# Sample attention of a decoder step: by kind of head, with gathered keys turned by DVE

## The chip, the cores and the metric

The kernel runs on one core of a Trainium2 chip. The metric is the device time of one execution in microseconds (us). A core has TensorE (PE in the profile, its weight loads PEld), VectorE (DVE), ScalarE (ACT), GpSimd (POOL) and SyncE (SP), which run their own instruction queues in order and meet at semaphores, and 16 DMA engines that all queues share. All data here is float32.

## The reference, cut to what matters

One layer of a decoder is applied to a prompt (256 tokens) and to 8 samples of 8 new tokens, each sample with 1024 past keys that lie in 8 pages of 128 tokens (a page table names them). Half of the attention is stick-breaking ("stick"), 8 heads of 64; half is differential ("diff"), 4 heads with two 64-wide key halves and values of 128. A mixture of experts (top 4 of 32) follows.

```python
# stick: z (heads, queries, keys), only keys before the query count
log_1m = where(mask, log_sigmoid(-z), 0.0)
log_rest = cumsum(log_1m, reverse=True) - log_1m
w = where(mask, exp(log_sigmoid(z) + log_rest), 0.0)      # = sigmoid(z_s) * product of sigmoid(-z_j), j > s
# diff: two softmaxes over z - slope * distance
a = p[:, 0] - lam * p[:, 1]
out = w_or_a @ v
```

The rest is projections, two layer norms, the router and, for each chosen expert, `gate_up` (1024 x 2048) and `down` (1024 x 1024).

## The kernel before, in words

The program is a row of blocks; at the end of each all engines meet.

**Block 1, projection** (L243 to L426). SP loads `w_in` into `ring`. PE projects the 64 sample rows and the first 128 prompt rows, then `turn(n)` (L310) transposes q and k rows of them, 8 turns of 4 transposes, ACT and DVE copying alternate turns out of banks 6 and 7 (`copy_turned`, L368; the sample queries go into `q_all`). Then PE projects the second prompt block (L329 to L332), which frees `ring` row by row (`w_in_used`), and turns that too. As `ring` comes free SP loads the first sample's pages (L255 to L258).

**Block 2, attention** (L486 to L1045). First the samples. One turn of the loop is one sample with both kinds. For each kind 1024 x 512 keys and as many values come as 16 page loads of 256 KB with 2 KB rows (`load_pages`, L208) into `slot[0]` to `slot[7]`, keys of stick in 0 and 1, of diff in 2 and 3, values in 4 to 7. PE transposes every 128x128 block of the keys (`turn_keys`, L583), ACT and DVE copy the results from banks 5 and 6 into `kT` (`copy_bank`, L487; `WHO` deals 22 bank copies per sample to the two), PE multiplies them by `q_now`, in which the queries of a head pair stand block-diagonal (`score_keys`, L597). Stick weights are made in logs: Abs, Exp, Ln on ACT (L794 to L797), max and add, a reversed scan of 1088 on DVE (L944), subtractions, Exp on ACT (L763). Diff weights are a biased maximum on DVE (L903 to L910) and Exp on ACT (L766). PE transposes the weights and multiplies them by the values (`mix_values`, L620, product L639), ACT copies the result, PE turns it (`turn_rows`, L645), DVE stores it into `mixT` (`store_rows`, L885). The order on PE is L660 to L671: the mix of the last sample lies between the key turns of this one. SP's order is L532. After the samples, L545 loads `w_out` and `load_weights` the first expert's weights, as slots come free. Then the prompt's attention runs in 6 units (L681 to L743, L819 to L861, L971 to L1045).

**Block 3** (L1131 to L1390) projects with `w_out`, norms, routes, and ranks tokens by expert. **Block 4** (L1451 on) runs 33 items of 64 slots: POOL gathers the item's rows (`gather`, L1470, 128 rows of 2 KB by indirect DMA), PE multiplies by the streamed weights of the expert (L1530, L1560) from the 12 slots, and SP loads the next expert's into each slot when `w_used` says that it is free.

## Time and profile before

| | us |
|---|---|
| Runs: median (lowest to highest of 3) | 1502.22 (1501.36 to 1503.99) |
| The profiled execution, its own time | 1504.01 |
| Its span, first to last instruction | 1502.2 |
| PE busy | 1317.1 (88%) |
| DVE, ACT, POOL busy | 475.0, 254.3, 56.2 |
| Mean granted TensorE clock | 0.928 of full speed |
| Block 1 | 0 to 135.9 |
| Samples' attention in block 2 | 136.4 to 344.2 |
| Prompt's attention, blocks 3 and 4 | to the end |

The profile gives for each engine what it was busy with and what ended its idle time. DMA rates are of the whole core. A PE row counts two instructions for each float32 product. A granted clock of 1.00 is 2.4 GHz and one of 0.50 is 1.2 GHz; a stretch between has some of both.

### The profile page before, as it was taken

How to read it: one execution, taken by the hardware profiler on the slowest of the kernel's cores; microseconds unless marked ns; L12 is line 12 of the kernel's file. 1: busy time of each engine (PE TensorE's matmuls, PEld its weight loads, DVE VectorE, ACT ScalarE, POOL GpSimd, SP SyncE). 2: the span in 40 equal slices, each digit the busy share in tenths (PEclk: the TensorE clock that was granted, in tenths of full speed). 3: DMA queues.
4: the chain of work that ended last, by engine and by line, in shares of the span. 5: the costliest groups of instructions: out<-in, count | busy, mean ns of one | idle time of the engine just before them, and what ended most of it. 6: DMA issues, size and time to landing. Idle time of an engine off the chain costs nothing.

```text
span 1502.2 us, 20503 instructions
## 1 busy us (share of the span) xinstructions
PE 1317.1 (88%) x7083; PEld 517.9 (34%) x7084; DVE 475.0 (32%) x809; ACT 254.3 (17%) x436; POOL 56.2 (4%) x90
## 2 busy tenths in 40 slices
PE   8997888874697999999899999999999999999994
PEld 3344555553344323222232222222322222222221
DVE  0002656565556221223222231222122222312225
ACT  0003666665422000000000000000000000000001
POOL 0000000000000000000000000000000000000000
PEclk9999999996595999999899999999999999999996
DMA  9144779896114999999999999599999999999991
GB/s 388 39 165 175 272 279 338 292 384 277 45 67 162 410 418 417 415 418 417 403 389 416 418 417 418 219 393 419 416 416 418 418 418 416 417 418 418 417 416 71
DMA packets 119411, 507.97 MB, mean 338 GB/s; under 512 B 13492, under 2 KB 13620, under 8 KB 85464
## 3 DMA queue, kind: packets, MB, share of 16 engines
q1 hardware_dynamic: 116016, 496.85, 82.9%
q0 software_dynamic: 3232, 10.49, 1.9%
q8 instruction: 16, 0.26, 0.1%
q10 hardware_dynamic: 136, 0.28, 0.0%
q14 instruction: 11, 0.09, 0.0%
HBM read 502.33 MB, written 5.24 MB: 338 GB/s over the span
## 4 chain that ended last, share of the span: by engine, by line
PE 53%; DVE 6%; DMA 4%; SPq 3%; ACT 1%; issue 1%; ACTq 0%; DVEq 0%; POOLq 0%; POOL 0%
PE psum L1530 28%; PE psum L1560 17%; PE psum L1500 6%; DMA arena<-in_w_gate_up 4%; SPq L226 3%; DVE arena L1680 1%; PE psum L1550 1%; ACT arena L1614 1%; DVE arena L1681 1%; DVE arena L1688 1%; DVE arena L1684 1%; PE psum L1509 1%; PE psum L1581 0%; DVE arena L1741 0%; DVE arena L1738 0%
## 5 line engine op out<-in xcount | busy, mean ns | idle before, releaser
L1530 PE MATMUL psum<-arena 128*64 128x512 f32 x2112 | 478.0, 599 | 4.7 <-issue 2.3
L1651 DVE SCALAR_TENSOR_TENSOR arena<-psum,arena 128x1024 f32<-128x1024 f32 (+2 forms) x132 | 128.0, 1008 | 592.5 <-PE psum L1500 592.1
L1560 PE MATMUL psum<-arena 128*64 128x512 f32 x1056 | 275.7, 682 | 22.7 <-ACT arena L1614 22.7
L1530 PEld LDWEIGHTS psum<-arena 128*64 128x64 f32 x2112 | 145.6, 137 | 326.1 <-issue 308.5
L1560 PEld LDWEIGHTS psum<-arena 128*64 128x64 f32 x1056 | 82.5, 155 | 195.0 <-issue 164.1
L1612 ACT ACTIVATE arena<-arena 128x512 f32<-128x512 f32 x33 | 20.8, 630 | 580.3 <-DVE arena L1680 580.3
L1500 PE MATMUL psum<-arena 64*128 64x512 f32 (+1 forms) x396 | 107.5, 632 | 0.9 <-ACT arena L1618 0.9
L593 PE MATMUL psum<-arena 128*128 128x128 f32 x512 | 74.4, 285 | 17.0 <-ACT arena L506 8.1
L283 PE MATMUL psum<-arena 128*128 128x512 f32 x192 | 85.9, 603 | 0.0
L506 ACT ACTIVATE arena<-psum 128x512 f32<-128x512 f32 x112 | 61.9, 574 | 69.6 <-PE psum L593 41.1
L1618 ACT ACTIVATE arena<-psum 128x512 f32<-128x512 f32 x33 | 19.7, 597 | 281.7 <-PE psum L1560 281.7
L593 PEld LDWEIGHTS psum<-arena 128*128 128x128 f32 x512 | 55.8, 143 | 32.3 <-ACT arena L506 14.1
L1680 DVE TENSOR_SCALAR arena<-psum 128x512 f32<-128x512 f32 x33 | 22.8, 692 | 137.8 <-PE psum L1530 137.8
L1509 PE MATMUL psum<-arena 1*64 1x512 f32 x272 | 37.0, 612 | 29.1 <-DVE arena L1681 28.2
L504 DVE COPY arena<-psum 128x512 f32<-128x512 f32 (+1 forms) x64 | 39.5, 639 | 66.7 <-PE psum L593 43.4
L1500 PEld LDWEIGHTS psum<-arena 64*128 64x128 f32 (+1 forms) x396 | 26.5, 167 | 79.4 <-issue 79.4
L283 PEld LDWEIGHTS psum<-arena 128*128 128x128 f32 x192 | 36.3, 193 | 49.5 <-issue 49.5
L351 DVE COPY arena<-psum 128x512 f32<-128x512 f32 (+2 forms) x18 | 11.2, 645 | 121.4 <-PE psum L335 41.7
L1471 POOL COPY small_i<-small_i 128x1 int32 (+1 forms) x34 | 6.2, 182 | 1056.9 <-PE psum L1492 886.4
L1474 POOL DMA_INDIRECT arena<-x_rows,small_i x34 | 40.2, 1183 | 26.8 <-POOL small_i L1471 26.8
L626 PE MATMUL psum<-arena 128*128 128x128 f32 x144 | 22.9, 286 | 15.4 <-ACT arena L763 11.3
L639 PE MATMUL psum<-arena 128*32 128x128 f32 x1152 | 36.2, 281 | 0.0
(197 smaller groups left out, 862.1 us busy)
## 6 DMA issues: line engine op xcount, KB each, us to landing
arena<-in_w_gate_up SPq DMA_DIRECT2D x256, 1024.0 KB, 17.0
arena<-in_w_down SPq DMA_DIRECT2D x128, 1024.0 KB, 13.9
arena<-in_cache_sb_k SPq DMA_DIRECT2D x64, 256.0 KB, 4.3
arena<-in_cache_diff_k SPq DMA_DIRECT2D x64, 256.0 KB, 8.0
arena<-in_cache_sb_v SPq DMA_DIRECT2D x64, 256.0 KB, 5.2
arena<-in_cache_diff_v SPq DMA_DIRECT2D x64, 256.0 KB, 6.9
arena<-in_w_in SPq DMA_DIRECT2D x8, 1536.0 KB, 20.2
arena<-in_w_out SPq DMA_DIRECT2D x4, 1024.0 KB, 18.1
```

The source lines that it names most:

```text
L226: sp.dma_start(dst, src).then_inc(w_loaded[s], 16)
L283: return nc.tensor.matmul(psum[:, bank_of[n], :], xT[:, k, b * P:(b + 1) * P], ring[:, col:col + 512], start=(k == 0), stop=(k == KD - 1))
L504: nc.vector.tensor_copy(dst, src).then_inc(copied["dve"], 1)
L506: nc.scalar.activation(dst, src, ACT.Copy).then_inc(copied["act"], 1)
L593: ins = nc.tensor.transpose(psum[:, 5 + j % 2, h * P:(h + 1) * P], slot[s][:, at:at + P], ident)
L1474: pool.indirect_dma_start(xg, None, x1_dram, bass.IndirectOffsetOnAxis(ap=idx_now, axis=0)).then_inc(gathered, 16)
L1500: ins = nc.tensor.matmul(psum[0:nt, banks[h], :], scatter[r, t0:t0 + nt], y_rows[r, :], start=True, stop=True)
L1509: ins = nc.tensor.matmul(psum[64 * h:64 * h + 64, n, :], ones_rows[32 * n:32 * n + 1, :], bias_row[32 * n:32 * n + 1, h * 512:h * 512 + 51 ...
L1530: ins = nc.tensor.matmul(psum[64 * h:64 * h + 64, n, :], x_k, slot[k][:, col:col + 512], start=False, stop=(k == KD - 1))
L1560: ins = nc.tensor.matmul(psum[64 * h:64 * h + 64, 4, :], h_k, slot[s][:, col:col + 512], start=(k == 0), stop=(k == KD - 1))
L1651: ins = nc.vector.scalar_tensor_tensor(out=r, in0=psum[0:nt, banks[h]:banks[h] + at_once, :], scalar=item_gate[0:nt, b, col], in1=r, op0=A ...
L1680: nc.vector.tensor_scalar(gate_in, psum[:, 0, :], LIMIT, None, ALU.min).then_inc(gate_clamped, 1)
```

## The change

The sample attention of block 2 is written anew, and block 1 prepares for it. The rest of the kernel is the same, except for a few constants in `consts` and places of buffers.

- **Units.** Instead of 8 turns with both kinds there are 16 units, `UNITS`: first 8 samples of stick, then 8 of diff. They are written out, not looped.
- **Keys.** A unit's keys (2 MB) come by one indirect DMA on POOL's queue, `load_keys`: 128 indices, each one contiguous run of 8 tokens, 16 KB, into one partition. Partition p then holds tokens 8p to 8p+7, so a block of 32 partitions holds a quarter of the keys. The indices are made in block 1 from the page table. There are two buffers, `K_raw`; unit u+2 is loaded after `keys_turned` says that u is turned.
- **Turning.** DVE transposes 32x32 blocks (`turn_keys(u, h)`: two instructions of 1024 elements per partition for each half h, four for a unit), from contiguous rows of 32, and writes them 8 elements (32 bytes) apart into `T`. PE's key transposes, the 16 bank copies and `kT` go.
- **Queries.** Block 1 spreads q and k of the samples over 32-row parts with products: sample turns n = 0 to 7 replace four turns of four transposes; a q turn has 32 products of 64 columns, a k turn 8. ACT's `place` puts them block-diagonal over the four quarters.
- **Scores** of a unit are 16 products of 264 columns (256 past and 8 own keys) in 2 banks, one for each h.
- **Stick weights.** ACT makes sigmoid(-z) and sigmoid(z) (4 instructions of 264); DVE scans the first as a product over 264 columns, twice; PE turns the quarters' totals, three small DVE operations multiply them up, PE turns them back, two DVE operations of 264 finish.
- **Diff weights.** The bias comes as a product; DVE takes the maximum, PE and DVE join it over the quarters, ACT takes Exp with the maximum as its bias.
- **Mixing.** 6 transposes instead of 9 and 36 products of 128 columns, as before. Values still come as 8 page loads with 2 KB rows on SP, two buffers; a unit's values load after the mix two units back.
- POOL makes the run indices in block 1 from 8 small DMAs of the page table; `w_out` is loaded at unit 4.

The core of it (the rest of the two kernels' block 2 is replaced in the same manner):

```diff
+        def load_keys(pool, u):
+            y, b = UNITS[u]
+            pool.indirect_dma_start(K_raw[u % 2], None, key_runs[y],
+                                    bass.IndirectOffsetOnAxis(ap=runs[:, b:b + 1], axis=0)).then_inc(keys_loaded[u % 2], 16)
...
                 def turn(n):
-                    b, i = (2, 0, 1)[n // 4], n % 4
-                    nt = BLOCKS[b][1]
-                    for h in range(4):
-                        ins = nc.tensor.transpose(psum[:, 6 + n % 2, h * P:h * P + nt],
...
+                    if n < 8:
+                        i = n // 2
+                        for j in range(8):
+                            at = i * 512 + 32 * (4 * (j // 2) + 2 * (n % 2) + j % 2)
+                            for c in range(3 * (i % 2), 4):
+                                ins = nc.tensor.matmul(psum[32 * c:32 * c + 32, 6 + n % 2, j * SAMPLES:(j + 1) * SAMPLES],
+                                                       qk_rows[0:64, 2, at:at + 32], ident[0:64, 0:64], start=True, stop=True)
...
-                for n in range(2, 8):
+                for n in range(2, 12):
...
             @block.sync
...
+                for u in range(2, N_UNITS):
+                    sp.wait_ge(mixed, u - 1)
+                    load_values(sp, u)
+                    load_own(u)
...
             @block.gpsimd
...
+                for u in range(2, N_UNITS):
+                    pool.wait_ge(keys_turned, 2 * u - 2)
+                    load_keys(pool, u)
...
             @block.tensor
...
+                score_unit(0, 0)
+                score_unit(0, 1)
+                for u in range(N_UNITS):
+                    if u + 1 < N_UNITS:
+                        score_unit(u + 1, 0)
+                    if u:
+                        turn_rows(u - 1)
+                    join_quarters(u)
+                    turn_weights(u)
+                    if u + 1 < N_UNITS:
+                        score_unit(u + 1, 1)
+                    mix_values(u)
+                turn_rows(N_UNITS - 1)
...
             @block.scalar
...
+                for u in range(N_UNITS):
+                    more = u + 1 < N_UNITS and UNITS[u + 1][0] == 0
+                    if UNITS[u][0]:
+                        exponents(u)
+                    if more:
+                        sigmoids(u + 1, 0)
+                    copy_weights(u)
+                    if more:
+                        sigmoids(u + 1, 1)
+                    if u + 2 < N_UNITS:
+                        place(u + 2)
+                    rows(u)
...
             @block.vector
...
+                def turn_keys(u, h):
+                    if h == 0:
+                        dve.wait_ge(keys_loaded[u % 2], 16 * (u // 2 + 1))
+                    if u:
+                        dve.wait_ge(scored, 2 * (u - 1) + h + 1)
+                    raw = K_raw[u % 2].rearrange("p (s g x r) -> p s g x r", s=RUN, g=4, x=4)
+                    turned = T[:, 8 * h:8 * h + 8, 0:QUARTER].rearrange("p (g d) (c s) -> p s g d c", d=2, s=RUN)
+                    for d in range(2):
+                        ins = nc.vector.transpose(turned[:, :, :, d, :], raw[:, :, :, 2 * h + d, :])
...
+                for u in range(N_UNITS):
+                    y = UNITS[u][0]
+                    if u + 1 < N_UNITS:
+                        turn_keys(u + 1, 0)
+                    if y == 0:
+                        sticks(u)
+                    else:
+                        maxima(u)
+                    if u:
+                        store_rows(u - 1)
+                    if u + 1 < N_UNITS:
+                        turn_keys(u + 1, 1)
+                    if y:
+                        factors(u)
+                store_rows(N_UNITS - 1)
```

## Rows read from the trace of the kernel before

**Rows 1.** The page: the chain that ended last, shares of the span.
```profile
PE 53%; DVE 6%; DMA 4%; SPq 3%; ACT 1%; issue 1%; ACTq 0%; DVEq 0%; POOLq 0%; POOL 0%
PE psum L1530 28%; PE psum L1560 17%; PE psum L1500 6%; DMA arena<-in_w_gate_up 4%; SPq L226 3%; DVE arena L1680 1%; PE psum L1550 1%; ACT arena L1614 1%; DVE arena L1681 1%; DVE arena L1688 1%; DVE arena L1684 1%; PE psum L1509 1%; PE psum L1581 0%; DVE arena L1741 0%; DVE arena L1738 0%
```

**Rows 2.** Time windows: span, busy us (and count) of PE, PEld, DVE, ACT, POOL, granted clock, DMA share, GB/s.
```profile
216.08:241.28 25.20, 20.54 (x277) 13.94 (x277) 14.23 (x26) 16.04 (x26) 0.40 (x1) 1.00 0.92 328
```

**Rows 3.** Timeline (start us, us, engine, line): the ends of the turns, projections and sample stage.
```profile
79.20 0.71 PE L315 MATMUL psum<-arena 64*128 64x64 f32 x8
...
86.45 42.55 PE L283 MATMUL psum<-arena 128*128 128x512 f32 x96
...
136.42 1.43 PEld L593 LDWEIGHTS psum<-arena 128*128 128x128 f32 x8 [2.90 <-issue]
...
216.08 2.04 PE L610 MATMUL psum<-arena 128*32 128x512 f32 x16
...
241.28 2.04 PE L610 MATMUL psum<-arena 128*32 128x512 f32 x16
...
344.04 0.19 DVE L896 TENSOR_TENSOR arena<-psum,arena 128x32 f32<-128x32 f32 x1
```

**Rows 4.** Groups by line and form, 0 to 560 us: xcount | busy us, mean ns | idle before.
```profile
L593 PE MATMUL psum<-arena 128*128 128x128 f32 x512 | 74.4, 285 | 17.0 <-ACT arena L506 8.1 <-issue 4.5 <-DVE arena L504 3.7
L506 ACT ACTIVATE arena<-psum 128x512 f32<-128x512 f32 x104 | 59.7, 597 | 66.3 <-PE psum L593 41.1 <-PE psum L626 25.1
...
L504 DVE COPY arena<-psum 128x512 f32<-128x512 f32 x56 | 38.0, 690 | 66.7 <-PE psum L593 43.4 <-PE psum L626 23.1
...
L944 DVE TENSOR_TENSOR_SCAN arena<-arena 128x1088 f32<-128x1088 f32 x8 | 19.4, 2426 | 0.3
...
L949 DVE TENSOR_TENSOR arena<-psum,arena 128x1024 f32<-128x1024 f32 x8 | 9.7, 1215 | 0.0
...
L994 DVE TENSOR_TENSOR_SCAN arena<-arena 128x256 f32<-128x256 f32 x8 | 4.9, 673 | 0.1
...
L837 ACT ACTIVATE arena<-arena 128x256 f32<-128x256 f32 x8 | 4.0, 496 | 3.9 <-DVE arena L1022 3.9
...
L1039 DVE SCALAR_TENSOR_TENSOR arena<-arena 128x256 f32<-128x256 f32 x4 | 1.8, 482 | 0.1
```

**Rows 5.** Timeline: one mix of 36 products; one round trip ACT, PE, DVE.
```profile
235.79 2.17 PE L639 MATMUL psum<-arena 128*32 128x128 f32 x72
...
343.45 0.33 PE L647 MATMUL psum<-arena 128*128 128x128 f32 x1 [0.49 <-ACT arena L757]
...
343.81 0.19 DVE L894 COPY arena<-psum 128x32 f32<-128x32 f32 x1 [2.55 <-PE psum L647]
```

**Rows 6.** Two single lines: strided and contiguous reductions of 256 elements.
```profile
L1667 DVE TENSOR_REDUCE arena<-arena x3: 590/600/609, 484.0 to 488.2; 128x64 f32<-128x256 f32 x2, 64x64 f32<-64x256 f32 x1
...
L1367 DVE TENSOR_REDUCE arena<-arena x3: 411/420/421, 466.3 to 471.6; 128x8 f32<-128x256 f32 x2, 64x8 f32<-64x256 f32 x1
```

**Rows 7.** DMA view, 165 to 318 us, in 40 slices: page loads.
```profile
GB/s 246 393 373 392 389 380 30 163 293 400 391 388 386 172 248 336 400 389 387 387 46 291 313 403 388 387 382 29 252 360 399 388 387 380 26 245 378 398 387 388
```

**Rows 8.** Windows while 8 KB rows are loaded: columns as in rows 2.
```profile
540.00:700.00 160.00, 150.72 (x678) 47.29 (x676) 40.01 (x54) 9.72 (x16) 6.85 (x10) 0.97 1.02 417
```

**Rows 9.** Chain in order of time: the first gather of rows.
```profile
477.88 3.19 DMA arena<-x_rows,small_i
```

**Rows 10.** Short windows around a fall and a rise of the clock: columns as in rows 2.
```profile
132.00:135.00 3.00, 1.51 (x11) 0.86 (x9) 1.79 (x4) 1.05 (x2) 0.00 (x0) 1.00 0.02 5
...
138.00:141.00 3.00, 2.22 (x12) 1.62 (x11) 0.11 (x1) 1.84 (x4) 0.55 (x2) 0.66 0.32 122
...
357.00:360.40 3.40, 2.94 (x14) 1.82 (x10) 2.81 (x7) 1.47 (x4) 0.00 (x0) 0.50 1.03 422
...
408.00:411.40 3.40, 3.40 (x12) 0.99 (x9) 0.00 (x0) 0.00 (x0) 0.00 (x0) 0.75 0.89 281
```

**Rows 11.** Timeline: one mix after the fall.
```profile
335.10 3.56 PE L639 MATMUL psum<-arena 128*32 128x128 f32 x72
```

More of the change, by code:

```diff
@@ L70, in constants @@
     put("pneg", np.where(k < 128 + i, 0.0, NEG))
[L72 to L73 removed]
+    c = (i % 32) // 8
+    group, quarter, q = i // 32, (i % 32) // 8, i % 8
+    n = np.arange(KEYS_Q)[None, :]
+    own = n >= QUARTER
     slope = np.array(SLOPES)[group]
[L75 to L80 removed]
+    key = np.where(own, PAST + n - QUARTER, QUARTER * quarter + n)
+    seen = np.where(own, (quarter == 3) & (n - QUARTER <= q), True)
+    put("abias", np.where(seen, slope * (key - (PAST + q)), NEG))
+    n = np.arange(DEC_T)[None, :]
+    put("smask", np.where((quarter == 3) & (n < q), 0.0, NEG))
+    row_c = (j % 32) // 8
+    put("fold", np.concatenate([(j // 32 == group) & (j % 8 == q) & (row_c % 2 == h) for h in range(2)], axis=1))
+    put("run", i % (PAGE // RUN))
+    put("minus", -1.0 * (i == np.arange(2)[None, :]))
     put("slot", j % SLOTS)
@@ new lines, in exponents @@
+                def exponents(u):
+                    b = UNITS[u][1]
+                    act.wait_ge(max_spread, b + 1)
+                    nc.scalar.activation(minus_max, psum[:, SIDE[u % 2], P:P + 2], ACT.Copy).then_inc(max_copied, 1)
+                    act.wait_ge(max_copied, b + 1)
+                    act.wait_ge(w_turned, u)
+                    for h in range(2):
+                        ins = nc.scalar.activation(W[u % 2][:, h, :], z_of(u, h), ACT.Exp, bias=minus_max[:, h:h + 1],
+                                                   accum_out=row_sum[:, h:h + 1])
+                        if h == 0:
+                            own.mark(ins)
+                    ins.then_inc(w_ready, 1)
+                    act.wait_ge(w_ready, u + 1)
+                    act.sem_inc(z_used, 1)
@@ new lines, in copy_weights, with rows @@
+                def copy_weights(u):
+                    act.wait_ge(w_turned, u + 1)
+                    if u >= 2:
+                        act.wait_ge(mixed, u - 1)
+                    own.mark(nc.scalar.activation(w_past[u % 2], psum[:, W_BANK, :], ACT.Copy))
+                    own.wait()
+                    nc.scalar.activation(w_own[u % 2][0:DEC_T, :], psum[0:DEC_T, SIDE[u % 2], 256:512], ACT.Copy
+                                         ).then_inc(w_copied, 1)
+                def rows(u):
+                    y, b = UNITS[u]
+                    act.wait_ge(mixed, u + 1)
+                    if u:
+                        act.wait_ge(o_turned, u)
@@ L805, in _ @@
-                turn(0, first=True)
-                own.leave(1)
-                with act.Fori(1, DEC_B) as b:
-                    turn(b)
-                    own.leave(DEC_B - 1)
-                skip("act", act, DEC_B, (0, 1, 2, 3))
-                weights(DEC_B - 1, 0)
-                banks("act", act, DEC_B, (4, 5, 6))
-                skip("act", act, DEC_B, (7, 8, 9, 10))
-                weights(DEC_B - 1, 1)
-                rows(DEC_B - 1, 0)
-                banks("act", act, DEC_B, (11, 12, 13))
@@ L817, in _, with place @@
-                rows(DEC_B - 1, 1)
+                    nc.scalar.activation(o_rows, psum[:, O_BANK, 0:P], ACT.Copy, scale=row_factor[:, 0:1] if y else 1.0
+                                         ).then_inc(o_copied, 1)
+                def place(u):
+                    y, b = UNITS[u]
+                    if u:
+                        act.wait_ge(scored, 2 * u)
+                    for i in range(4):
+                        r = slice(32 * i, 32 * i + 32)
+                        nc.scalar.activation(q_blocks[u % 2][r, :, 8 * i:8 * i + 8], spread[r, 2 * y, :, 8 * b:8 * b + 8],
+                                             ACT.Copy).then_inc(blocks_ready, 1)
+                    nc.scalar.activation(T[96:128, :, QUARTER:KEYS_Q], spread[96:128, 2 * y + 1, :, 8 * b:8 * b + 8], ACT.Copy
+                                         ).then_inc(blocks_ready, 1)
```

664 lines of the change are left out of this document (273 added, 391 removed).

## The prediction

> **What bounds it now.** I read the page's chain first. It names only lines of block 4 [rows 1]: from there on the core lives on streamed weights, at 417 GB/s with PE busy 94% of the time [rows 8]. The change does not touch that work, and its start is the end of what lies before. So the question is how long blocks 1 and 2 take; whatever the samples' attention gains or loses moves everything behind it by as much, since the first expert's weights and `w_out` come long before they are used.
>
> The timeline gives the stage: turns from 79.20, the second projection from 86.45, the samples' attention from 136.4 to 344.2 [rows 3]. One sample takes 241.28 - 216.08 = 25.2 us [rows 3], so one kind of one sample, a unit of the new kernel, takes 12.6. The window of that turn has PE busy 20.5 of 25.2 us, ACT 16.0, DVE 14.2, DMA 0.92 at 328 GB/s [rows 2]. PE is the longest, and its idle time and the copies' are waits on each other: the key and weight transposes L593 (74.4 us in the stage) wait for ACT and DVE bank copies, which wait for the transposes [rows 4]. DMA is near behind: loads run at about 390 GB/s where they run, with holes between the bursts [rows 7].
>
> A measurement of this kernel can tell about 0.2% (3 us) from no change.
>
> **What goes.** Per sample 64 key transposes on PE (74.4 us over 8 samples, 9.3 each), the 16 key bank copies of 0.60 to 0.69 us on ACT and DVE, the scan of 2.43 us, and the log arithmetic [rows 4]. What stays per unit on PE: scores, 16 products of 264 columns instead of 8 of 512, so the same 2.04 us as L610 [rows 3]; the mix, 36 products, 2.17 us as L639 [rows 5]; 6 transposes and side products, 1.3; sum with round trips about 6.5 us against some 10 before.
>
> **What comes on DVE.** A unit has 4 transposes of 1024 elements. No row shows one. Below: a one-pass operation of 1024 took 1.22 us (L949) [rows 4], so t = 1.22. Above: the slowest rate per element in the trace is the scan's, 2426 ns for 1088 [rows 4], so about 2.3 us. I take t = 1.25 with 1.9 as the near worry: reading with steps of 256 bytes cost L1667 600 ns where L1367, contiguous, took 420 for the same 256 elements [rows 6], 0.7 ns more per element, which on 1024 gives 1.9; the transpose writes in steps of 32 bytes, but reads rows, so it is nearer to the contiguous row. A stick unit has besides two scans of 264 (673 ns for 256, so 1.4), two round trips to PE of 0.4 us each (PE's L647 starts at 343.45, DVE's next at 343.81), three small operations of 0.2, two operations of 0.45 and two small stores [rows 4, 5]: 1.4 + 0.8 + 0.6 + 0.9 + 0.4, with gaps 4.3 us. DVE needs 4t + 4.3 = 9.3 us for a stick unit. A diff unit has a maximum over 528 (0.7), a round trip, two small operations, stores and factors, about 2.5, so 4t + 2.5 = 7.5.
>
> The Trainium skill ("Vector Engine (DVE) Microarchitecture Reference", The reshape front-end) says that the transpose sustains one element per cycle per lane. By it t is at the lower end; no run yet shows it.
>
> **PE in that loop.** In a stick unit PE has, from the moment the keys' second half is turned: scores 1.0, mix 2.2, scores of the next unit's first half 1.0, row transpose 0.3, and only then the quarter totals, at about 5.0; DVE could ask for them at 2.5 + 1.4 = 3.9. So DVE waits about 1 us and the loop is near 10.3. In a diff unit the chain maximum, join, Exp (two of 0.5, L837 [rows 4]), transposes 1.3, two ACT copies of about 1.0 and factors takes DVE from one unit to the next in about 9.5. ACT itself has 4 to 5 us of work in either.
>
> **What the loads allow.** A unit is 2.1 MB of keys and 2.1 MB of values. Values still have 2 KB rows, at 390 GB/s [rows 7] 5.4 us. For runs of 16 KB there is no row: the 8 KB rows of the weights went at 417 GB/s [rows 8], 5.0 us. The bytes alone give 10.4 us per unit. But the load is also a loop: keys of u+2 are issued when u is turned, and DVE's next transpose needs them one period later. The gather of 256 KB landed 3.2 us after its issue [rows 9], 0.6 of it data, after about 1 us of POOL, so some 3.6 us are fixed. With 5.0 for the data if nothing else runs, and 10.0 if values take half throughout, a period lies between 8.6 and 13.6. Values start some 3 to 4 us after the keys are issued, when PE has mixed; keys have had 1 us or so alone and share the rest, which gives 11.3 in a stick unit and up to 12.4 in a diff unit if the two queues share evenly, 10.4 if keys get more. I take P = 11.5 for a unit.
>
> **Block 1.** Eight sample turns take the place of four. A q turn has 32 products of 64 columns. The nearest row, L639's 72 instructions in 2.17 us, 30 ns each [rows 5], gives 64 instructions 1.9 us; a k turn, 8 products on one group, is like the 8 instructions of L315 in 0.71 [rows 3], twice, 1.4. That is 4 x 1.9 + 4 x 1.4 = 13.2 us for what took about 4 with its waits, so +9, between +4 (some of it under copies) and +14 (the clock low, as it was for part of 138 to 141 [rows 10]). It is all on the path: PE does the turns before the second projection, and no loads can start before that. The 8 small table loads on POOL lie under `w_in`'s load, where PE is busy; nothing, and 2 us if they hold back the first x rows. The removed clearing of `v_new` is hidden too.
>
> **The sum,** against the profiled execution's own 1504.0 (span 1502.2; 1.8 above the median of the runs). The stage begins at 136.4 + 9 = 145.4. DVE turns unit 0 (4t = 4.9), and iteration 0 starts at 150. It takes 10, then 14 iterations of P, then the last unit from its turned keys: scores 1.2, maximum and join 1.7, Exp 1.8, transposes 1.3, copies 1.0, mix 2.2, rows and store 1.2 = 10.4. 150 + 10 + 14 x 11.5 + 10.4 = 331.4, against 344.2: 12.8 less. 1502.2 - 12.8 = 1489.4 as a median, say 1489. The break-even period is P = 12.4.
>
> **Rivals.**
> *Loads at full rate.* If the gather's long runs go first where the queues share, P is 10.5, and the stage ends at 150 + 10 + 147 + 10.4 = 317.4, 26.8 less: 1475. For it: values have nearly two periods of slack, keys one. Against: nothing in the trace shows two big streams at once. With block 1 at +4 it would be 1470. Chance 0.23.
>
> *The transposes are slow* (slower than before). At t = 2.3 DVE needs 13.5 for a stick unit and 11.7 for a diff unit, seven of each in the middle 176; the start is 4.3 later and iteration 0 two longer: 150 + 4.3 + 12 + 176.4 + 10.4 = 353, 9 more: 1511. At t = 1.9 it is 11.9 and 11.5 (loads) and hardly moves the forecast. The balance is at t = 2.1. For it: the strided row [rows 6]. Against: that row strides its reads. Chance 0.14.
> The Trainium skill ("Advanced Engine Details and Errata", SBUF Cachelines) says that accesses that go to another 16-byte line each time are slower; steps of 32 bytes do that. By this rule t is above 1.22; row L1667 agrees for reads, at 1.7 times per element; for writes no row shows it.
>
> *The clock falls in the stage* (slower). Before, PE was busy 81% and had 1.00 throughout [rows 2]. It fell after PE had been busy half the time (132 to 135, then 0.66), and stayed at 0.50 while busy 2.94 of 3.4; it rose only after a fully busy stretch [rows 10]. In the new stage PE is busy some 6.5 of 11.5 us. At 0.50 the mix takes 3.56 instead of 2.17 [rows 5, 11] and scores a microsecond more each half; in a stick unit PE then comes to the totals at 8.5 instead of 5, and the period is about 13. 150 + 11 + 182 + 12 = 355, 11 more: 1513. For it: those rows. Against: gaps in the loop are under 2 us each, and the loop has a microsecond or two of slack under the loads. A partly low clock stays inside the forecast. Chance 0.12.
>
> *The gather does not keep up* (the change doesn't do what it says): if runs of 16 KB share with values from the start, P = 13.6, and 150 + 10 + 190 + 10.4 = 361, 17 more: 1519. Chance 0.07.
>
> **Numbers.** The forecast, P of 11 to 12, has 0.44 and runs from 1482 to 1497. The range takes it, the fast case and most of the two slow ones up to P = 13: 1467 to 1513. Slower by over 0.2% holds most of the three slow cases: 0.28. Within 0.2%: 0.06. Faster 0.66.
>
> **What would show it.** Transposes near 1.25 us each, 64 of them; DVE waiting for keys (DMA) once per unit, not for PE; stage periods of 11.5 in both kinds, about equal; DMA share above 0.9 with no holes of 30 GB/s; the second projection starting near 95 instead of 86.45; blocks 3 and 4 unchanged in length. The forecast is wrong if units of the two kinds differ by more than 1.5 us (then an engine's chain sets them), if a transpose is above 2 us, if the granted clock is near 0.50 in the stage, or if the gathers land later than 10 us after issue.

## The result and the profile after

The changed kernel takes 1538.8 us in the median of four runs (1532.2 to 1544.0) beside 1503.1 of the kernel before on the same chip: 1.0235 times as long, 95% interval 1.0215 to 1.0254. The forecast was 1489, the range 1467 to 1513. It is slower, by 36 us, where 14 us less were foretold. The profiled execution has a span of 1533.2, 31.0 more than before. TensorE's first product of the prompt starts at 376.69 us; before it was 343.71, and the sample stage ended near 344.2 [rows 3]. So all of it lies ahead of there, in the sample stage and block 1.

The page's chain looks as it did [rows 1], with nothing of the stage in it; the groups say more (page, line, engine, out<-in, count | busy us, mean ns | idle before):

```profile
L836 DVE STREAM_TRANSPOSE arena<-arena 128x1024 f32<-128x1024 f32 x64 | 123.0, 2019 | 2.8 <-DVE arena L920 1.3
...
L550 PE MATMUL psum<-arena 128*32 128x264 f32 x512 | 50.9, 532 | 38.8 <-DVE arena L836 31.5
...
L605 PE MATMUL psum<-arena 128*16 128x128 f32 x1024 | 46.6, 359 | 11.6 <-issue 10.4
```

The 64 transposes take 2.02 us each, not 1.25; TensorE waits 31.5 us for them. The timeline of one stick unit, from one group of transposes to the next:

```profile
203.23 7.59 DVE L836 STREAM_TRANSPOSE arena<-arena 128x1024 f32<-128x1024 f32 x4 [0.16 <-DVE arena L920]
...
206.12 4.47 SPq L220 DMA_DIRECT2D arena<-in_cache_sb_v  x8
207.22 1.99 PE L550 MATMUL psum<-arena 128*32 128x264 f32 x16 [3.54 <-DVE arena L836]
...
209.66 2.79 PE L605 MATMUL psum<-arena 128*16 128x128 f32 x64
...
212.72 1.10 PE L550 MATMUL psum<-arena 128*32 128x264 f32 x16
...
214.51 0.18 DVE L872 COPY arena<-psum 2x32 f32<-2x32 f32 x1 [2.60 <-PE psum L562]
...
216.91 2.02 DVE L836 STREAM_TRANSPOSE arena<-arena 128x1024 f32<-128x1024 f32 x1 [0.16 <-DVE arena L920]
```

It is a ring through two engines. Two transposes (3.8 us) must end before TensorE can score the second half, and it is idle 3.54 us until then. Behind that wait the same 16 score products take 1.99 us that take 1.10 a few microseconds later, and the mix takes 2.79 where it took 2.17 before [rows 5] and takes 1.94 in this kernel at the full clock (below). VectorE in turn waits 2.60 us for the quarter totals. The windows of this unit and of the whole stage (columns as in [rows 2]):

```profile
203.23:216.91 13.68, 8.28 (x120) 4.94 (x118) 10.40 (x14) 4.05 (x12) 0.94 (x1) 0.75 0.74 278
```
```profile
144.00:360.00 216.00, 138.55 (x1737) 81.86 (x1737) 156.49 (x189) 64.16 (x194) 14.19 (x17) 0.73 0.77 289
```

The granted clock is a mean of 0.73 of its upper level (2.4 GHz) over the stage, so it spends a good half of it at 1.2 GHz; the loads run 0.77 of the time at 289 GB/s. Before it was 1.00 and 0.92 [rows 2]. Neither an engine nor the loads are busy throughout: in a stick unit the ring of waits is the bound.

A third loss stands out in the order of units. Their periods, from the own-key product of one mix to the next, are 13.8, 13.7, 13.7, 13.7, 23.2, 14.0, 13.7 for the stick units, and 10.3 to 14.5 for the softmax ones. The timeline around the long one, SyncE's queue and TensorE:

```profile
194.65 0.71 SPq L499 DMA_DIRECT2D arena<-arena  x1
206.12 4.47 SPq L220 DMA_DIRECT2D arena<-in_cache_sb_v  x8
210.63 0.73 SPq L499 DMA_DIRECT2D arena<-arena  x1
211.41 4.04 SPq L514 DMA_DIRECT2D arena<-in_w_out  x4
225.63 5.85 SPq L220 DMA_DIRECT2D arena<-in_cache_sb_v  x8
```
```profile
236.49 0.60 PE L553 MATMUL psum<-arena 128*128 128x8 f32 x2
245.99 1.27 PE L605 MATMUL psum<-arena 128*16 128x128 f32 x20 [8.90 <-issue]
```

Values of the sixth unit are issued at 225.63, behind 4 MB of `w_out`, and TensorE stands 8.90 us. While it stands the loads run at 404 GB/s (window 225.6 to 246), so it waits for bytes that were asked for late. And the line that reads the page numbers into SyncE's registers, which the forecast did not price (line view, ns min/median/max):

```profile
L216 SPq TENSOR_LOAD <-in_page_table_ptr x16: 1003/2500/4477, 116.3 to 353.5; - x16
L216 SPq TENSOR_LOAD <-in_page_table x16: 873/886/3728, 118.7 to 355.5; - x16
```

They stand behind the wait for the mix. The third mix frees its tile at 199.1 us and the values are issued at 206.12; for the next three units issue comes 12.8, 13.2 and 4.3 us after the mix. Of the 12.8, SyncE spends 2.7 on the end of `w_out`'s issue (to 215.45) and 7.8 in these two loads (4.03 and 3.73). The start of the stage (timeline, all engines):

```profile
143.97 7.57 DVE L836 STREAM_TRANSPOSE arena<-arena 128x1024 f32<-128x1024 f32 x4 [0.32 <-PEq L250]
...
149.66 1.99 PE L550 MATMUL psum<-arena 128*32 128x264 f32 x16 [7.33 <-ACT arena L758]
...
153.16 3.85 DVE L836 STREAM_TRANSPOSE arena<-arena 128x1024 f32<-128x1024 f32 x2 [0.23 <-DVE arena L853]
...
157.17 1.99 PE L550 MATMUL psum<-arena 128*32 128x264 f32 x16 [3.02 <-DVE arena L836]
...
171.24 0.41 PE L609 MATMUL psum<-arena 8*16 8x128 f32 x8
```

From the first transpose to the end of the first mix pass 27.7 us, with nothing of another unit to overlap. Last, block 1 (timeline):

```profile
16.93 1.98 PE L299 MATMUL psum<-arena 128*64 128x512 f32 x4 [5.06 <-DMA arena<-in_w_in]
```

The first product with `w_in` starts at 16.93; before it was 12.14. The sample turns start at 83.17 (79.20 in [rows 3]) and the second projection at 95.49 (86.45).

### The profile page after: what moved, and what is told of

Same layout as the page of the kernel before. It is cut to its first block, busy times and chain, and to the rows that moved or that the text cites. A ratio compares the mean times of both kernels' runs of the same rounds, so it can differ in the third digit from the quotient of the medians.

```text
span 1533.2 us, 19561 instructions
## 1 busy us (share of the span) xinstructions
PE 1305.1 (85%) x7091; PEld 500.1 (33%) x7092; DVE 520.8 (34%) x804; ACT 192.2 (13%) x418; POOL 71.5 (5%) x108
## 4 chain that ended last, share of the span: by engine, by line
PE 52%; DVE 6%; DMA 4%; SPq 3%; ACT 1%; issue 1%; DVEq 0%; POOLq 0%; POOL 0%; ACTq 0%
PE psum L1503 27%; PE psum L1533 16%; PE psum L1473 6%; DMA arena<-in_w_gate_up 3%; SPq L233 3%; DVE arena L1653 1%; PE psum L1523 1%; ACT arena L1587 1%; DVE arena L1654 1%; DVE arena L1661 1%; DVE arena L1657 1%; PE psum L1482 1%; PE psum L1554 1%; DVE arena L1714 0%; DVE arena L1711 0%
## 5 line engine op out<-in xcount | busy, mean ns | idle before, releaser
L1503 PEld LDWEIGHTS psum<-arena 128*64 128x64 f32 x2112 | 145.4, 137 | 324.6 <-issue 309.7
L836 DVE STREAM_TRANSPOSE arena<-arena 128x1024 f32<-128x1024 f32 x64 | 123.0, 2019 | 2.8 <-DVE arena L920 1.3
L550 PE MATMUL psum<-arena 128*32 128x264 f32 x512 | 50.9, 532 | 38.8 <-DVE arena L836 31.5
L605 PE MATMUL psum<-arena 128*16 128x128 f32 x1024 | 46.6, 359 | 11.6 <-issue 10.4
L363 DVE COPY arena<-psum 128x512 f32<-128x512 f32 (+3 forms) x18 | 11.8, 677 | 126.6 <-PE psum L299 41.3
L1591 ACT ACTIVATE arena<-psum 128x512 f32<-128x512 f32 x33 | 19.7, 598 | 280.0 <-PE psum L1533 280.0
L289 PEld LDWEIGHTS psum<-arena 128*128 128x128 f32 x192 | 35.8, 190 | 48.1 <-issue 48.1
L605 PEld LDWEIGHTS psum<-arena 128*16 128x16 f32 x1024 | 37.1, 129 | 22.8 <-issue 15.8
L550 PEld LDWEIGHTS psum<-arena 128*32 128x32 f32 x512 | 17.2, 137 | 61.4 <-issue 38.6
L584 PE MATMUL psum<-arena 128*128 128x128 f32 x64 | 14.7, 326 | 20.7 <-ACT arena L720 11.9
## 6 DMA issues: line engine op xcount, KB each, us to landing
arena<-in_w_down SPq DMA_DIRECT2D x128, 1024.0 KB, 14.1
```

The source lines that it names most:

```text
L289: return nc.tensor.matmul(psum[:, bank_of[n], :], xT[:, k, b * P:(b + 1) * P], ring[:, col:col + 512], start=(k == 0), stop=(k == KD - 1))
L550: ins = nc.tensor.matmul(z_of(u, h)[32 * g:32 * g + 32, :], q_blocks[u % 2][:, j, :], T[:, j, :], start=(y == 0 and d == 0), stop=(y == 1 ...
L605: nc.tensor.matmul(psum[32 * g:32 * g + 16, O_BANK, 0:P], w_past[n][:, r:r + 16], V_raw[n][:, pg * 512 + g * P:pg * 512 + (g + 1) * P], st ...
L836: ins = nc.vector.transpose(turned[:, :, :, d, :], raw[:, :, :, 2 * h + d, :])
L1503: ins = nc.tensor.matmul(psum[64 * h:64 * h + 64, n, :], x_k, slot[k][:, col:col + 512], start=False, stop=(k == KD - 1))
```

## Experiments

Sixteen kernels ran. E is the changed kernel, 1538.8 us. All are medians; each was measured beside the kernel before, which was between 1501.9 and 1503.0, and a bracket with two ratios is the 95% interval of the time over that. E's own is 1.0215 to 1.0254. Differences whose intervals overlap are not shown by the times alone.

**What a transpose costs.** Added once, behind the last unit's scores, e.g.:

```diff
+ own.link(nc.vector.transpose(wide[:, 0:1024], src))
...
+ own.link(nc.vector.transpose(wide[:, 0:1024].rearrange("p (a c s) -> p a s c", a=4, s=8),
+                              src.rearrange("p (a b r) -> p a b r", a=4, b=8)))
```

> The changed kernel with nine VectorE operations added once, in the 16th unit, on 128 x 1024 floats, each waiting for the one before and writing to a tile that nobody reads any more; nothing that is computed changes. They are: (1, 2) a 32x32-block transpose with dense read and dense write, twice; (3) with the elements of a written row 2 floats apart; (4) 4 apart; (5) 8 apart with two blocks interleaved in each destination; (6) 8 apart with all eight interleaved, as the kernel's own; (7) a dense write with a read 8 apart; (8) a dense copy; (9) a copy in the layout of (6). If the step of the writes is what made the transposes slow: (1, 2) near 1.1 us, a rise with the step up to 2.0 us at (5) and (6), (7) near 1.1 to 1.25, and (9) slower than (8) too. If the transpose of 32x32 blocks of floats is slow by itself: (1) to (7) all near 2.0 us, and (8, 9) below 1.25. If the interleaving of eight blocks costs, not the step: (5) well below (6). Time: some 10 to 15 us above the changed kernel, near 1550.

One run, 1548.5 us. The timeline on VectorE, (1) to (9) in order:

```profile
365.37 1.25 DVE L897 STREAM_TRANSPOSE arena<-arena 128x1024 f32<-128x1024 f32 x1 [1.89 <-PE psum L550]
366.66 1.25 DVE L898 STREAM_TRANSPOSE arena<-arena 128x1024 f32<-128x1024 f32 x1
367.94 1.25 DVE L899 STREAM_TRANSPOSE arena<-arena 128x1024 f32<-128x1024 f32 x1
369.22 1.98 DVE L900 STREAM_TRANSPOSE arena<-arena 128x1024 f32<-128x1024 f32 x1
371.23 2.02 DVE L901 STREAM_TRANSPOSE arena<-arena 128x1024 f32<-128x1024 f32 x1
373.29 2.01 DVE L902 STREAM_TRANSPOSE arena<-arena 128x1024 f32<-128x1024 f32 x1
375.33 2.01 DVE L903 STREAM_TRANSPOSE arena<-arena 128x1024 f32<-128x1024 f32 x1
377.37 0.70 DVE L904 COPY arena<-arena 128x1024 f32<-128x1024 f32 x1
378.10 1.09 DVE L905 COPY arena<-arena 128x1024 f32<-128x1024 f32 x1
```

Dense, 1.25 us. With a step of 2 floats (8 bytes) the same; with 4 floats (16 bytes) 1.98, and 8 cost no more than 4. Interleaving does not matter ((5) and (6) agree), and, against what was expected, a stepped read (7) costs as much as a stepped write. The copy pays too, 1.09 for 0.70. So it is the step, on either side. On the written side 8 bytes are free and 16 are not; on the read side only 32 were tried. The Trainium skill ("Advanced Engine Details and Errata", SBUF Cachelines) speaks of 16-byte lines of which two accesses are needed for full speed: the trace agrees, with 8 bytes free and 16 bytes dear, for writes too. The Trainium skill gives "one element per cycle per lane" for the transpose ("Vector Engine (DVE) Microarchitecture Reference", The reshape front-end); the trace does not bear it out for every layout, with 1.25 us for 1024 elements dense and 1.98 to 2.02 stepped.

**Dense keys, three ways.** The tile holds column s*33 + c in place of 8*c + s, own keys at c = 32:

```diff
- turned = T[:, 8 * h:8 * h + 8, 0:QUARTER].rearrange("p (g d) (c s) -> p s g d c", d=2, s=RUN)
+ turned = T[:, 8 * h:8 * h + 8, :].rearrange("p (g d) (s c) -> p s g d c", d=2, s=RUN)[:, :, :, :, 0:32]
```

In the first kernel TensorE undoes the order as it reads: `T[:, j, :].rearrange("p (s c) -> p c s", s=RUN)`.

> The tile of turned keys holds column s*33 + c in place of 8*c + s, so that the transposes write 32 floats in a row, and the score products read the tile with a step of 33 floats; the computation is the same. If the 8-float step of the writes made the transposes slow: from 1.98 us to between 1.1 and 1.25 us, two of four in a row end 1.7 us earlier, TensorE's idle time of 3.5 us before the second half of the scores shrinks to under 2, a stick unit goes from 13.7 us to about 11.5 to 12, and the time is 1517 to 1526 us. If the transposes are slow whatever the step: they stay at 1.98 and the time within 2 us of 1538. If TensorE reads the stepped tile slower, its score halves go over 1.99 us and eat the gain: time 1530 or more with fast transposes. If the loads bound the stage, the DMA share is at 0.95 or more and the units stay near 13 us with fast transposes.

1535.6 us (1.0205 to 1.0245), 3 us less than E, which is no difference beside the intervals. Transposes and scores (line view, then the timeline):

```profile
L836 DVE STREAM_TRANSPOSE arena<-arena x64: 1202/1205/1249, 143.2 to 353.8; 128x1024 f32<-128x1024 f32 x64
```
```profile
203.67 2.15 PE L550 MATMUL psum<-arena 128*32 128x264 f32 x16 [2.07 <-DVE arena L836]
...
209.51 2.11 PE L550 MATMUL psum<-arena 128*32 128x264 f32 x16
```

The transposes are at 1.205, but the step has moved to TensorE: its 32 score halves take 67.7 us, 2.12 each at either clock, where those of E take 50.9 (1.10 or 1.99 each). The unit is still 13.6 us. So the step goes to the engine that can take it, ScalarE, whose sigmoids read the scores from a bank:

```diff
- nc.scalar.activation(keep[:, h, :], z_of(u, h), ACT.Sigmoid, scale=-1.0)
+ nc.scalar.activation(by_run(keep[:, h, :]), z_in_order(u, h), ACT.Sigmoid, scale=-1.0)
```

> The changed kernel with the dense layout and ScalarE's stepped reads alone, w_out where the change has it. e5_dense_z, which also loads w_out last, stands 26 us under the changed kernel, and the late w_out alone 10 us. If the two add up: 16 us under the changed kernel, 1521 to 1525 us, with one long unit of 22 us or more. If faster units only run into the same late values: 1528 or more.

1525.7 us (1.0136 to 1.0171): 13 us less than E. The sigmoids take 392 ns (391 in E), a read of a bank in steps of 33 floats is free here. Units: 13.0, 11.8, 13.9, 13.0, 24.5, 13.0, 12.7, and 10.0 to 13.9. With `w_out` last:

> Two edits of the changed kernel: the turned keys in the layout s*33 + c, and w_out loaded after the last values. Unlike the earlier dense version TensorE reads the tile in a row, so the scores come out in that order, and ScalarE's two sigmoids (and the exponentials) read them from the bank with a step of 33 floats and write them in the order of the keys; the computation is the same. If the 2.11 us of a score half in the earlier dense version came from TensorE's stepped read: it is back at 1.10 us at the full clock (1.99 behind a wait), the transposes stay at 1.2, a stick unit takes 12.0 to 12.6 us, and the time is 1514 to 1521 us. If ScalarE reads a bank with such a step slower: its sigmoids go over 0.39 us and give back up to 1 us a unit: 1521 to 1527. If the loads bind the stage beside this: DMA share over 0.9 and 12.7 us or more a unit with idle TensorE and VectorE before keys or values: 1524 to 1528.

1512.6 us (1.0048 to 1.0089), but from 1509.0 to 1523.4 between runs; the profiled one has a unit of 20.6 us in the softmax half, where the mix waited 7.24 us for values that SyncE issued late.

**Where `w_out` stands.** On E alone, `if u == 4:` becomes `if u == N_UNITS - 1:`.

> The four 1 MB loads of w_out are issued after the values of the last unit in place of after those of the fifth; the computation is the same. If they stood ahead of the values of the sixth unit and made the one stall of 9.6 us (237 to 246 us): that unit goes from 23.3 us to near 13.7, the later ones keep 11 to 14, and the time is 1528 to 1531 us. If the stage is bound by the bytes that it loads: the units get longer elsewhere and the time stays within 2 us of 1538. If the second block then waits for w_out, its start moves later and gives back up to 10 us: time 1538 or more.

1528.6 us (1.0149 to 1.0203), 10 us less; all seven stick periods are 13.5 to 13.8.

**Page numbers.** First read earlier, still from DRAM, on e5_dense_z:

```diff
+ pages = page_numbers(u)
  sp.wait_ge(mixed, u - 1)
- load_values(sp, u)
+ load_values(sp, u, pages)
```

> The same as e5_dense_z with the eight page numbers of a unit's values read into SyncE's registers before its wait for the mix and not behind it. If that reading, 4 to 7 us behind the wait, makes the values late: they are issued within 1 us of the mix that frees their tile, the mixes of the softmax units wait less for them, and the time is 3 to 10 us under e5_dense_z. If the values land in time anyway or the bytes bind: within 2 us of it.

1510.7 us (1.0037 to 1.0070; runs 1509.3 to 1514.6): 2 us less than e5_dense_z, which a measurement cannot tell from nothing, though no unit of its profile is over 13.0. The values were not issued within 1 us of the mix, as the expectation had it, but 0.2 to 9.8 us after it: SyncE issues the eight loads (4 to 5 us), then reads the next numbers (3.1 and 1.4 us in the median), and that fills its time in a unit. Then loaded once into SBUF, alone on E:

```diff
+ sp.dma_start(small_i[0:1, 0:64], a["page_table"]...).then_inc(numbers_loaded, 16)
...
- a["page_table"][b:b + 1, :], engines=[mybir.EngineType.SP], min_val=0,
+ small_i[0:1, 8 * b:8 * b + 8], engines=[mybir.EngineType.SP], min_val=0,
```

> The changed kernel with the page numbers read from SBUF alone. If the register loads behind the wait are half of the stall of 9.6 us: the values of a unit are issued 3 to 5 us earlier, the unit of 23.3 us falls to 18 to 20, and the time is 1531 to 1536 us. If w_out ahead of the values is the whole of it: within 2 us of 1538.

1525.1 us (1.0139 to 1.0176), 13.7 us less than E: more than expected, and as much as the dense keys. Values are issued 3.0 to 6.0 us after the mix, in E 4.3 to 13.2. The loads to registers (line view) and SyncE's timeline:

```profile
L217 SPq TENSOR_LOAD <-small_i x16: 532/692/988, 116.1 to 342.9; - x16
```
```profile
200.28 4.67 SPq L221 DMA_DIRECT2D arena<-in_cache_sb_v  x8
...
205.76 1.95 SPq L518 DMA_DIRECT2D arena<-in_w_out  x4
213.52 9.16 SPq L221 DMA_DIRECT2D arena<-in_cache_sb_v  x8
```

One load of 0.7 us takes the place of two that sum to 3.4 in the median and to 8 at worst. Values of the sixth unit are issued from 213.52, not 225.63, and with `w_out` still ahead of them the long unit is 15.6 us, not 23.2. So `w_out` and the late issue made the stall together: with `w_out` last the unit takes 13.7, with values asked for earlier 15.6. An estimate: 4 MB are 10 us of loading at the rate of [rows 8], and early values can wait them out. The Trainium skill ("DMA: Bandwidth & Descriptors", Latency and other measured facts) has a floor of about 600 ns for such a register load. The traces do not bear it out as a floor: from SBUF the least here is 532, and in block 4 of E SyncE's line L1430 takes 275 ns in the median of 31. From DRAM in the busy stage the first of the two takes 2500.

**The clock.** Products that nobody reads fill TensorE's wait in each stick unit:

```diff
  turn_weights(u)
+ if u < 8:
+     for _ in range(8):
+         nc.tensor.matmul(psum[:, 2 * ((u + 1) % 2) + 1, KEYS_Q:BANK], ident, tab[:, 0:BANK - KEYS_Q], ...)
  if u + 1 < N_UNITS:
      score_unit(u + 1, 1)
```

> Eight products of 128x128 with 248 columns that nobody reads are added on TensorE in each of the eight stick units, where it waits for the second half of the turned keys; they write an unused part of a bank. If the falling clock behind that wait costs time: the granted clock in the stick units goes from 0.75 to 1.00, the mix from 2.79 to 2.17 us, the score half from 1.99 to near 1.1, the unit from 13.7 to 12 to 12.7 us, and the time is 1526 to 1532 us. If VectorE alone sets the unit: the clock rises, the units stay at 13.7 and the time within 2 us of 1538. If the added products run into the arrival of the keys, the units get longer by up to 1 us each: 1540 to 1546.

1535.7 us (1.0202 to 1.0263), no gain: the clock rose (0.87 in the stick stretch), scores and mix took 1.10 and 1.94 us, but eight were too many:

```profile
203.36 5.20 PE L629 MATMUL psum<-arena 128*128 128x248 f32 x16
208.49 1.10 PE L550 MATMUL psum<-arena 128*32 128x264 f32 x16
```

They end at 208.5; the keys, whose transposes began at 203.07, were ready near 207. With five:

> The changed kernel with five added products in each stick unit in place of eight, nothing else. The eight took 5.2 us in a wait of 3.5 us and made the scores about 1.6 us late. If the clock theory holds: the five take 3.2 us and end with the wait, the score half takes 1.1 us, the mix 1.94 us, the stick unit 11.7 to 12.1 us (from 13.7), and the time is 1525 to 1530 us. If the loads bind at that pace: the units stay over 12.5 us and the time over 1532.

1532.6 us (1.0161 to 1.0232), 6 us less than E in the median, with intervals that overlap. The units show the gain, 12.0 to 12.3 us in place of 13.7, until the values are late; then come 14.1 and 27.5. On e5_dense_z, three:

> The same as e5_dense_z with three products of 128x128 with 248 columns added in each of the eight stick units where TensorE waits for the second half of the turned keys; nobody reads them. If the clock behind that wait still costs time: the score half at 1.1 in place of 1.99, the mix at 1.94 in place of 2.8, a stick unit 1.0 to 1.8 us shorter than without them, near 11 us, and the time 7 to 12 us under e5_dense_z, about 1508. If the loads bind by then: the units go no lower than those of e5_dense_z, with the DMA share over 0.9, and the time stays within 3 us of it.

1516.6 us (1507.7 to 1523.3), inconclusive: units of 11.1 and 11.0, then 14.2, and one of 21.6 in the softmax half.

**Block 1.** The small table loads on POOL after `w_in`, on e8_early: `pool.wait_ge(w_sem[KD - 1], 16)` ahead of them.

> The same as e8_early (dense turned keys, w_out last, page numbers read early), and POOL issues its eight small loads of the page table only when the last part of w_in has landed. In the changed kernel's trace the first product with w_in starts at 16.93 us and not at 12.14 as before, the loads move 160 GB/s in the first 10 us and not 285, and SyncE needs 6.99 us and not 4.33 to issue w_in. If the page-table loads do that: the first product is back near 12.2 us, the turns of the sample rows start near 79 us in place of 84, and the time is 4 to 5 us under e8_early's, near 1506. If it is something else in the first block: no difference, and the time within 2 us of e8_early's 1510.7.

```profile
79.20 5.56 PE L329 MATMUL psum<-arena 64*32 64x64 f32 x260
```

The turns start at 79.20, as before the change, 4.8 us earlier than in e8_early. The first 10 us load 288 GB/s (160 in E). The median, 1509.1, gained only 1.6, less than the intervals can tell, with runs between 1501.9 and 1515.9. In the profiled one, the slowest, units of 16.2, 13.8 and 14.0 us gave it back. Then fewer, larger turns (on e8_early; a q turn's 32 products become 8, from a fourfold copy of the queries):

```diff
- for c in range(3 * (i % 2), 4):
-     ins = nc.tensor.matmul(psum[32 * c:32 * c + 32, ...], qk_rows[0:64, 2, at:at + 32], ident[0:64, 0:64], ...)
+ src = qk_rows[0:64, 2, at:at + 32] if i % 2 else q_four[0:64, 4 * at - 1024 * i:4 * at - 1024 * i + P]
+ ins = nc.tensor.matmul(psum[96 * (i % 2):128, ...], src, ident[0:64, 0:64], ...)
```

> The same as e8_early, and the queries of the samples are copied four times side by side (one copy each by ScalarE and VectorE behind their copies of the projection, beside other products), so that one product of 64x128 writes all four quarters where four of 64x32 did: 96 of the 160 small products that spread the sample rows go. If the number of small products sets their time: the stretch from the end of the first projection to the start of the second goes from 12.3 to 13.9 us to near 8, and the time is 4 to 6 us under e8_early's. If the wait for the copies behind them sets it: less than 2 us.

1522.1 us (1.0116 to 1.0153), 11 slower than e8_early:

```profile
84.13 16.05 PE L331 MATMUL psum<-arena 64*128 64x64 f32 x128
```

This row merges two forms. By form (line view, 84 to 100.2 us), and the granted clock of a part (window, columns as in [rows 2]):

```profile
L331 PE MATMUL psum<-arena 64*128 64x64 f32 x64 | 10.6, 341 | 0.0
L331 PE MATMUL psum<-arena 64*32 64x64 f32 x64 | 5.6, 264 | 0.0
```
```profile
92.00:96.00 4.00, 4.00 (x20) 4.00 (x20) 0.00 (x0) 0.60 (x1) 0.00 (x0) 0.50 0.00 0
```

Only the q turns have 128 stationary columns. At the full clock such a turn (16 instructions) takes 2.0 us; in e8_early its 64 instructions of 32 columns, on four column groups in turn, take 1.1. A k turn (16 of 32 columns, one group) takes 1.1 us in both. From about 90 us on the clock is 0.50, and a wide q turn takes 3.6, a k turn 1.9. In e8_early the clock falls there too (its 320 instructions take 10.6 us, in E at 1.00 only 8.65), so both the wider product and the clock are in the difference, 5.8 us up to the second projection. The number of instructions was not the cost. The other half of the 11 is not explained.

> Both of the edits, the late page-table loads and the four-fold queries, on e8_early. If the parts of the first block add up: 9 to 10 us under e8_early's, 1500 to 1502 us, which is at or just below the kernel before, since the stage behind it is then of the same length as before's within 2 us. If block 1 was not on the path: within 2 us of e8_early's.

1519.5 us (1.0085 to 1.0117): the wide turns lose it again, 18.3 us for the same 128 instructions, with the clock at 0.50 from 84 to 102 us.

> The same as e11_both with three added products in each stick unit, as in e6_dense_warm. There a unit took as little as 11.0 us, but 14.1 at times, at a DMA share of 0.86. If the clock still binds the stick units: 3 to 8 us under e11_both, below the kernel before. If the loads bind them: within 2 us of e11_both, with the mean of the units over 12 us.

1516.7 us (1510.2 to 1525.8): unclear, again single units of 15.1 and 17.3 between others of 9.9 to 12.5.

**All together.** Dense keys, `w_out` last, late table loads, page numbers from SBUF and read ahead of the wait (no wide turns):

> The same as e9_table_late, but the 64 page numbers are loaded once into SBUF, and SyncE reads its registers from there and not from DRAM. In e9_table_late SyncE's two register loads per unit take 3.24 and 1.55 us in the median and 5.40 and 4.57 at most, which with 4.4 to 5.6 us for issuing the values leaves little of a unit of 12.7. If they make the values late and are what scatters the times (1502 to 1516): each is under 1 us, the values are issued right behind the mix that frees them, no unit of the stage goes over 14.5 us, the scatter falls to a few us and the time is 1500 to 1505. If the loads' own rate makes the long units: they stay, and the time is within 2 us of 1509.

1503.5 us, 0.9998 to 1.0018 of before; eleven runs between 1502.5 and 1507.9, where the same kernel with the numbers from DRAM scattered by 14. No unit is over 13.8, and each unit's values are issued 0.2 us after the mix, where e9_table_late had 0.2 to 13.8. The windows of its stick and softmax halves:

```profile
168.49:256.41 87.92, 62.57 (x823) 36.75 (x819) 52.93 (x90) 27.75 (x80) 6.58 (x7) 0.73 0.95 333
256.41:348.82 92.41, 73.96 (x945) 46.12 (x941) 43.54 (x81) 30.95 (x95) 4.70 (x5) 0.78 0.94 350
```

> The same as e13_sbuf_pages with three added products in each stick unit. If the clock binds the stick units once the values come in time: they go from about 12.5 to 11 us and the time is 5 to 10 us under e13_sbuf_pages, below the kernel before. If the loads bind at that pace: less than 3 us under it, with the DMA share over 0.9.

1495.6 us, 0.9932 to 0.9967 of before: the first version that is faster than it. Stick half:

```profile
163.98:246.31 82.33, 66.98 (x866) 43.29 (x862) 52.83 (x90) 27.90 (x82) 6.57 (x7) 0.81 0.96 349
```

Now that values come in time the added products bring 7.9 us in the medians, although the loads stand at 0.96: seven stick periods take 82.3 us where they took 87.9. Not all of the 7.9 need be theirs. In the two profiled executions the stage ends 9.4 us apart, and 4.2 of that stand in block 1, which the edit does not touch. There the clock fell behind the small turns in the one and not in the other (windows, e13_sbuf_pages and then e14_sbuf_warm):

```profile
80.00:137.00 57.00, 55.62 (x406) 30.67 (x394) 5.15 (x9) 4.25 (x8) 4.18 (x6) 0.91 0.47 166
80.00:137.00 57.00, 53.60 (x434) 28.87 (x422) 7.16 (x11) 6.15 (x11) 4.18 (x6) 1.00 0.47 167
```

## Why the prediction was wrong

**The step that failed first** is the price of the transposes, "I take t = 1.25", with the argument that "the transpose writes in steps of 32 bytes, but reads rows, so it is nearer to the contiguous row". It took 2.02, and dense 1.205 to 1.25 (four in a row 7.6 and 4.6 us). The term was right for a layout that the change does not have; the strided row [rows 6], whose 0.7 ns per element gave the "near worry" of 1.9, was the row to take (its 600 ns against 420 is 1.4 times, though, not the 1.7 of the text). The dense layout alone is worth 13.1 us.

**The loop was taken too loosely.** Even at t = 1.9 the text had a stick unit at 11.9, and "it hardly moves the forecast"; by its 4t + 4.3 it would be 12.4 at 2.02, and it was 13.7. Two rivals were weighed apart that are one mechanism: slow transposes make TensorE wait 3.5 us, behind that wait its clock is down, and scores and mix are 0.9 and 0.85 us longer on the path than at the full clock. The rows said so [rows 10, 11], but "gaps in the loop are under 2 us each" was worked out with the wrong t. The added products show it: stick units of 12.0 to 12.3 us with them alone, and the stick half of the last version 5.6 us shorter.

**The start of the stage was mis-sized.** The sum has 4.9 us for turning unit 0 and 10 for iteration 0, from 145.4 to 160. That part took 27.7 in E and still 25.7 in the last version. The scores of unit 0 (4.5 us) are not in the sum, and in iteration 0 the turns and scores of unit 1 follow one another with nothing of another unit beneath: TensorE waits 3.02 and 2.33 us for transposes. This is read from the trace; no run changed this part. With it the stage adds up: it ended at 377.2 and not at 331.4, 45.8 us later, of which the start has 11.6, the 14 periods 33.0 (the long unit 9.6, the pace of the stick units 15.6, of the softmax units 7.8) and the last unit 1.2.

**A wait that was never in the sum.** Values were granted "nearly two periods of slack" and their issue nothing. SyncE's register loads behind the wait for `mixed` took 3.4 us and up to 8, and `w_out` was put ahead of one unit's values. This loss is as large as that of the layout, 13.7 us for the loads alone, 10.2 for `w_out` alone. Both act on the same long unit (23.2 us, then 15.6 and 13.7), so they cannot add in full.

**Block 1 came out at +9.0, as forecast, by two errors.** The second projection started at 95.49, "near 95". But the turns took 12.3 us in place of 7.25, +5.1 and not +9. The rest is the page table's small loads, which were priced at "nothing, and 2 us if they hold back the first x rows": they held back the first product by 4.8, of which 4.0 were left at the turns. The agreement of the sum is luck. At the start of the stage it is +7.6 (143.97 against 136.42). What the text gave as the +14 case, a low clock, did come in other executions: in e8_early the turns took 13.9.

**What held.** The bytes: with values in time the last version runs both kinds of unit at 11.8 and 11.6 us a unit (82.3 over 7, 93.1 over 8) at a share of 0.93 to 0.96, where P = 11.5 and "both about equal" was forecast. VectorE never waited for a gather, though most of them landed later than the 10 us that the text named as a sign of being wrong (8.1 to 12.4 in E). Of its other signs a transpose above 2 us came true, and with the long unit the two kinds differ by 2.5 us (15.1 and 12.6 in the mean). From the first product of the prompt to the end it is 1156.5 us, 1158.5 before, so blocks 3 and 4 held. The whole gap of the changed kernel to the last version is 43.2 us; the parts taken alone (13.1, 13.7, 6.2, 10.2, and the 4.8 of block 1, which is from a trace) sum to 48.0. Two of them share a stall, but an excess of 4.8 us is also within what such medians scatter, with E's own runs 12 apart; which it is, is not shown.

Not settled: what alternates the last version's stick units between 12.5 and 11.4 us, whether its start and its 9 us of small turns in block 1 can go another way, and in what share of executions the clock falls behind those turns.

## What to carry to other kernels

Price a transpose, or a copy, with the stride of its output, not only of its input; if a step of 16 bytes or more (as these traces have it) must be somewhere, let the engine with slack take it, and measure that it does (here ScalarE's read of a bank, not TensorE's read of SBUF). For every DMA with a computed address count the register loads ahead of it, and keep the numbers in SBUF. Price the first unit of a pipeline by itself, since nothing overlaps there. And when a total agrees, check its parts: +9 came out of two errors.

## What the runs showed of the hardware

- VectorE on 128 x 1024 floats: transpose 1.25 us dense or with writes in steps of 8 bytes, 1.98 with writes in steps of 16, 2.01 to 2.02 with writes or reads in steps of 32; copy 0.70 dense and 1.09 with writes in steps of 32.
- TensorE, 16 products of 264 columns read from SBUF in steps of 132 bytes: 2.05 to 2.18 us at either clock, in place of 1.10 at the full clock and 1.99 at half. ScalarE reading a bank in such steps: 392 ns, 391 dense.
- Register loads by SyncE: from SBUF 0.69 us in the busy stage of e16_sbuf_only, 1.0 in e13_sbuf_pages, 0.28 in block 4 of E; 2.5 plus 0.9 in the median from DRAM, to 4.5 plus 3.7, under loads of some 300 GB/s.
- Eight loads in 4-byte words, issued by POOL beside `w_in`, brought the first 10 us from 285 to 160 GB/s, and the first product 4.8 us later.
- Small products of 64 rows and 64 moving columns at a granted clock of 1.00: 64 instructions of 32 stationary columns on four column groups in turn 1.1 us, 16 of 32 columns on one group 1.1 us, 16 of 128 columns 2.0 us; at 0.50 the last two take 1.9 and 3.6 us.
